# A gated-delta scan stage reordered on five engines, with one multiply moved from GpSimd to VectorE

## What is computed

```python
q = l2_norm(q) * K ** -0.5 ; k = l2_norm(k)
decay  = exp(where(incl, gcum_i - gcum_j, -inf))
a      = where(strict, (k * beta) @ k.T * decay, 0)
sol    = triangular_solve(I + a, [v * beta, k * beta * exp(gcum)])   # u, w
attn   = (q @ k.T) * decay
q_dec  = q * exp(gcum) ; k_end = k * exp(gcum_last - gcum)
# over the chunks, S = 0 at first
v_new = u - w @ S
o     = q_dec @ S + attn @ v_new
S     = S * chunk_decay + k_end.T @ v_new
```

## Time and profile before

| | us |
|---|---|
| median of 3 runs (3778.26 to 3779.26) | 3778.9 |
| the profiled execution | 3775.26 |
| its span, first to last instruction | 3773.5 |
| busy in the span: PE / DVE / ACT / POOL | 3565.7 / 1966.6 / 1510.6 / 471.2 |

### The profile page before, as it was taken

How to read it: one execution, slowest core, us unless ns; L and a number is a source line. 1 busy time by engine, 2 the same in 40 slices (tenths; PEclk the granted TensorE clock), 3 DMA queues, 4 the chain that set the end, 5 groups by cost and what they waited for, 6 DMA issues and landing times. The chain is left out here.

```text
span 3773.5 us, 49646 instructions
## 1 busy us (share of the span) xinstructions
PE 3565.7 (94%) x19794; PEld 2959.4 (78%) x19794; DVE 1966.6 (52%) x2979; ACT 1510.6 (40%) x2532; POOL 471.2 (12%) x362
## 2 busy tenths in 40 slices
PE   6999999899776789999999999999999999999998
PEld 4688888787655668888888788888888888888886
DVE  7455555467566634755455553436533444454543
ACT  3322222254644443565565642324222444442332
POOL 1000000134211000011011160120000000025021
PEclk8999999999988899999999999999999999999999
DMA  9734323332533336422223163335634555543332
GB/s 360 260 131 137 114 95 103 96 98 59 180 107 92 97 119 195 126 84 87 86 74 93 54 201 98 95 90 103 132 115 124 123 94 111 111 128 101 93 95 89
DMA packets 580503, 448.37 MB, mean 119 GB/s; under 512 B 64454, under 2 KB 500114, under 8 KB 579504
## 3 DMA queue, kind: packets, MB, share of 16 engines
q1 hardware_dynamic: 572080, 421.18, 39.6%
q10 hardware_dynamic: 6048, 19.14, 1.3%
q0 software_dynamic: 2144, 4.87, 0.4%
HBM read 387.61 MB, written 57.46 MB: 118 GB/s over the span
## 5 line engine op out<-in xcount | busy, mean ns | idle before, releaser
L2379 DVE TENSOR_TENSOR w_lo<-w,w_hi 128x512 fp32r<-128x512 f32 x429 | 291.3, 698 | 500.1 <-ACT w_hi L2372 499.9
L2372 ACT ACTIVATE w_hi<-w 128x512 fp32r<-128x512 f32 x429 | 260.9, 625 | 478.0 <-PE od_acc L2358 171.1
L4511 DVE TENSOR_TENSOR w_lo<-w,w_hi 128x512 fp32r<-128x512 f32 x260 | 232.2, 899 | 353.6 <-ACT w_hi L4404 352.2
L4370 PE MATMUL ta_acc<-u_hi,w_hi 128*128 128x512 f32 x960 | 375.2, 391 | 2.8 <-POOL u_lo L4305 1.4
L4372 PE MATMUL ta_acc<-u_hi,w_lo 128*128 128x512 f32 x960 | 373.6, 389 | 0.0
L4371 PE MATMUL ta_acc<-u_lo,w_hi 128*128 128x512 f32 x960 | 373.5, 389 | 0.0
L4404 ACT ACTIVATE w_hi<-w 128x512 fp32r<-128x512 f32 x260 | 163.5, 630 | 440.8 <-PE ta_acc L4372 433.9
L2356 PE MATMUL od_acc<-u_hi,w_hi 128*128 128x512 f32 x768 | 304.7, 397 | 0.0
L2358 PE MATMUL od_acc<-u_hi,w_lo 128*128 128x512 f32 x768 | 299.3, 390 | 0.0
L2357 PE MATMUL od_acc<-u_lo,w_hi 128*128 128x512 f32 x768 | 299.0, 389 | 0.0
L2356 PE MATMUL ev_acc<-u_hi,w_hi 128*128 128x512 f32 x608 | 250.3, 412 | 14.7 <-DVE w_lo L2379 5.1
(11 more groups left out here) (754 smaller groups left out, 8062.4 us busy)
## 6 DMA issues: line engine op xcount, KB each, us to landing
w<-in_o_w_in_dram SPq DMA_DIRECT2D x260, 256.0 KB, 6.6
w<-in_e_w_in_dram SPq DMA_DIRECT2D x144, 256.0 KB, 2.9
p_w<-in_w_in_dram SPq DMA_DIRECT2D x70, 512.0 KB, 6.2
mod_w<-in_w_ada_dram SPq DMA_DIRECT2D x32, 1024.0 KB, 11.8
w<-in_ple_gate_w_dram SPq DMA_DIRECT2D x128, 256.0 KB, 2.7
gate_w<-in_w_ada_dram SPq DMA_DIRECT2D x16, 1024.0 KB, 5.7
z_w<-in_w_in_dram SPq DMA_DIRECT2D x64, 256.0 KB, 2.9
w<-in_e_w_out_dram SPq DMA_DIRECT2D x64, 256.0 KB, 2.7
```

The costliest lines, as they stand in the source:

```text
L2372: act.activation(self.w_hi[m % self.ring][:], self.w[m % self.ring][:], ACT.Copy).then_inc(self.hi_set, 1)
L2379: eng.tensor_tensor(self.w_lo[m % self.ring][:], self.w[m % self.ring][:], self.w_hi[m % self.ring][:].bitcast(F32), ALU.subtract).then_in ...
L4370: pe.matmul(bank, hi, hi_x[:, k, :], start=(k == 0), stop=False)
L4511: dve.tensor_tensor(self.w_lo[m % RING][:], self.w[m % RING][:], self.w_hi[m % RING][:].bitcast(F32), ALU.subtract).then_inc(self.lo_set, 1)
```

## The change

The arithmetic stays the same. What changes is the place of instructions in the lists and the engine of one multiply:

- SyncE: in the opening, `scatter_in(0)` stands ahead of `gather(2)`; in each round, the q loads stand ahead of `blocks_load`.
- TensorE: in the solve, `q_sums` goes behind `level6_t`, `finish` behind `turn_v(a)`. `k_sums` goes from ahead of the scan into its step 1; queries and products of `a` from steps 2 and 3 to 3 and 4, those of `b` from step 4 to 5, and the last products of `b` behind the scan.
- ScalarE: `square_q`, `ln_q`, `norm_ln`, `norm_exp` go one place or two later in the solve, `square_k` ahead of `queries` and `inverse_q`; in the scan `decay` goes later and `turn_tri` from step 4 to step 3.
- VectorE: 18 instead of 14 triangle steps ahead of the scan, 10 instead of 6 of them ahead of `finish`; in the scan `norm_k`, `attention`, `decayed` and `turned` go later by a slot or more.
- The query multiply (`queries`, two per pair) goes from GpSimd to VectorE. The mask addition stays on GpSimd, with nothing but `identity` ahead of it in a round.

```diff
@@ -203,7 +203,7 @@
...
         TRI_STEPS = B32 - 1
-        TRI_EARLY = 14
+        TRI_EARLY = 18
         MIX_SOLVED = 56
...
@@ -343,8 +343,8 @@
...
             scatter_out(0)
+            scatter_in(0)
             gather(2)
-            scatter_in(0)
             gather(3)
...
@@ -352,13 +352,13 @@
...
                 a, b = 2 * j + 4, 2 * j + 5
+                if ahead:
+                    load_q(a)
+                    load_q(b)
                 if more:
...
                     tail.load_weights(sp, len(tail.chunks))
-                if ahead:
-                    load_q(a)
-                    load_q(b)
                 if more:
...
@@ -547,16 +547,17 @@
...
                     if ahead:
-                        if n == 2:
+                        if n == 1:
+                            k_sums(a)
+                            k_sums(b)
+                        if n == 3:
                             queries(a)
                             products(a, range(0, 4))
-                        if n == 3:
+                        if n == 4:
                             products(a, range(4, CHUNKS))
-                        if n == 4:
+                        if n == 5:
                             queries(b)
                             products(b, range(0, 4))
-                        if n == 5:
-                            products(b, range(4, CHUNKS))
                     if not more and n in (2, 4):
...
@@ -641,31 +642,30 @@
...
                 level5_y(j)
-                if ahead:
-                    q_sums(a + 2)
-                    q_sums(b + 2)
                 if more:
...
                 level6_t(j, 1)
-                if j > 0:
-                    finish(j - 1)
+                if ahead:
+                    q_sums(a + 2)
+                    q_sums(b + 2)
                 level6_y(j, 0)
...
                     tail.pe_steps(pe, TAIL)
+                if j > 0:
+                    finish(j - 1)
                 weights(j, 0)
...
                 weights(j, 1)
+                steps(j)
                 if ahead:
-                    k_sums(a + 2)
-                    k_sums(b + 2)
-                steps(j)
+                    products(b + 2, range(4, CHUNKS))
                 if more and not ahead:
...
@@ -792,11 +792,10 @@
...
                             inverse_k(a)
-                            decay(a, range(0, 3))
                         if n == 1:
...
                             inverse_k(b)
-                            decay(a, range(3, 6))
+                            decay(a, range(0, 2))
                     for d in range(2):
...
@@ -810,10 +809,10 @@
...
                         if n == 2:
-                            decay(b, range(0, 3))
-                        if n == 3:
-                            decay(b, range(3, 6))
-                    if j + 1 < PAIRS and n == 4:
+                            decay(a, range(2, 6))
+                        if n == 4:
+                            decay(b, range(0, 6))
+                    if j + 1 < PAIRS and n == 3:
                         turn_tri(j + 1)
...
@@ -900,21 +899,19 @@
...
                     tail_job(2)
-                if ahead:
-                    square_q(a + 2)
-                    square_q(b + 2)
                 level5_y(j)
...
                 if ahead:
+                    square_q(a + 2)
+                    square_q(b + 2)
+                level6_t(j, 0)
+                level6_t(j, 1)
+                if ahead:
                     ln_q(a + 2)
                     ln_q(b + 2)
-                level6_t(j, 0)
-                level6_t(j, 1)
-                if j > 0:
-                    norm_ln(j - 1)
                 level6_y(j, 0)
...
@@ -922,20 +919,22 @@
...
                 if j > 0:
-                    norm_exp(j - 1)
+                    norm_ln(j - 1)
                 weights(j, 0)
...
                     copy_v(b)
+                if j > 0:
+                    norm_exp(j - 1)
                 weights(j, 1)
                 if ahead:
-                    inverse_q(a + 2)
-                    inverse_q(b + 2)
+                    square_k(a + 2)
+                    square_k(b + 2)
                 if more:
...
                 if ahead:
-                    square_k(a + 2)
-                    square_k(b + 2)
+                    inverse_q(a + 2)
+                    inverse_q(b + 2)
                 steps(j)
...
@@ -951,12 +950,6 @@
...
 
-            def queries(hd):
-                pool.wait_ge(q_normed, hd + 1)
-                pool.wait_ge(qdec_exp, hd + 1)
-                pool.tensor_tensor(qdec[hd % 4][:], qdec[hd % 4][:], q_n[hd % 4].rearrange("p (c q) -> p c q", c=LC).unsqueeze(2)
-                                   .to_broadcast([P, LC, 2, P]), ALU.mult).then_inc(q_decayed, 1)
-
             def identity(j):
...
@@ -968,15 +961,11 @@
...
             identity(0)
-            queries(0)
-            queries(1)
             for n in range(MIX_JOBS):
...
                     identity(j + 1)
-                    queries(2 * j + 2)
-                    queries(2 * j + 3)
                 if j + 2 < PAIRS:
...
@@ -1003,6 +992,12 @@
...
                 dve.tensor_tensor(q_n[hd % 4], q_n[hd % 4], sq_q[hd % 2][:], ALU.mult).then_inc(q_normed, 1)
+
+            def queries(hd):
+                dve.wait_ge(q_normed, hd + 1)
+                dve.wait_ge(qdec_exp, hd + 1)
+                dve.tensor_tensor(qdec[hd % 4][:], qdec[hd % 4][:], q_n[hd % 4].rearrange("p (c q) -> p c q", c=LC).unsqueeze(2)
+                                  .to_broadcast([P, LC, 2, P]), ALU.mult).then_inc(q_decayed, 1)
 
...
@@ -1066,20 +1061,22 @@
...
                             if ahead and slot == 1:
-                                if n == 0 and d == 1:
+                                if n == 1 and d == 1:
                                     norm_k(a)
-                                if n == 1 and d == 1:
+                                if n == 2 and d == 0:
                                     norm_k(b)
-                                if n == 2 and d == 1:
+                                if n == 3 and d == 0:
                                     attention(a)
-                                if n == 3:
-                                    decayed(a, d)
+                                if n == 3 and d == 1:
+                                    decayed(a, 0)
                                 if n == 4 and d == 0:
+                                    decayed(a, 1)
+                                if n == 4 and d == 1:
                                     turned(a)
-                                if n == 4 and d == 1:
+                                if n == 5 and d == 0:
                                     attention(b)
-                                if n == 5:
-                                    decayed(b, d)
+                                if n == 5 and d == 1:
+                                    decayed(b, 0)
                             if slot == 0 and n < CHUNKS - 1:
...
@@ -1102,6 +1099,7 @@
...
                 if ahead:
+                    decayed(b, 1)
                     turned(b)
...
@@ -1131,6 +1129,8 @@
...
             mix.split_low(dve, mix.ring)
+            for hd in range(2):
+                queries(hd)
             for n in range(TRI_STEPS):
...
@@ -1157,14 +1157,17 @@
...
                     tail.split_low(dve, 6)
-                for n in range(6 if more else 0):
+                for n in range(10 if more else 0):
                     triangle(j + 1, n)
...
                     tail.split_low(dve, len(tail.chunks))
-                for n in range(6, TRI_EARLY if more else 0):
+                for n in range(10, TRI_EARLY if more else 0):
                     triangle(j + 1, n)
+                if more:
+                    queries(2 * j + 2)
+                    queries(2 * j + 3)
                 if ahead:
```

## The result

The changed kernel takes 3758.9 us (median of six runs, 3752.2 to 3764.5), the kernel before beside it 3779.0 (six runs). The ratio is 0.9949, with a 95% interval of 0.9936 to 0.9961. It is faster by 0.5%, and the interval lies clear of 1. The forecast was 3759.5.

What follows compares the result with a forecast made beforehand. The prediction took VectorE, last to reach the first state copies, as setting the stage's pace. Terms -1.0 - 9.8 - 2 x 5.3 + 2 = -19.4 from 3775.3 gave 3755.9, plus 3.6 for the median: 3759.5 us, range 3744 to 3773.

Steps and rivals of the forecast that it cites:

- first pair, C (absolute): End of the first pair's second state copy, predicted at 1117.4 against 1118.4 before: -1.0 us.
- C: Time point: the end of the second state copy of a pair's scan.
- second pair, T to C: Second pair up to its state copies: predicted 41.6 us against 51.4 before, -9.8.
- T: Time point: the first level-5 product of a pair on TensorE.
- scan, first and second pair: From C to the next T: predicted 33.5 us against 38.8, 5.3 gained in each of two pairs, between 0 and 7.
- third pair: Pair without mask additions: about 0.5 us worse from VectorE's work, 1.5 more from turn_tri ahead of v_end; together +2.
- The opening: Scatter ahead of gather: TensorE's first product 2 us earlier, but the first pair's triangle about 4.6 us later through queued entries.
- the hold lies mostly in a wait: Second pair: GpSimd's mask additions, expected T + 17 to T + 24, fall mostly while VectorE awaits the output norm.
- the end hangs on `turned(a)`: Rival: the scan doesn't shorten, since its end hangs on the block chain started by turned(a); 3770 us, chance 0.16.
- the additions hold nothing: Rival: the mask additions fall where VectorE is idle in both pairs; 3751.6 us, chance 0.13.
- ScalarE becomes late inside the scan: Rival: turn_tri and decay queue ahead of v_end and v_new, 10 us in each of two pairs; 3790 us, chance 0.06.
- waits only change their names: Rival: TensorE idles for VectorE as long as it did for ScalarE; 3779 us, chance 0.05.

Runs made afterwards that it cites:

- k_sums_back: Changed kernel with only the key sums put back ahead of the scan on TensorE; 3758.5 us.
- mask_out: Changed kernel with GpSimd's four mask additions of heads 4 to 7 shrunk to one chunk and two columns, so their mask is left out; 3745.6 us.
- open_old: Changed kernel with the opening's old queue order, the gather of the third head ahead of the first scatter; 3751.0 us.
- best_b: best_a with the old opening order too, gather of the third head ahead of the first scatter; 3736.0 us.
- best_a: Changed kernel with 14 early triangle steps, mask additions on VectorE, and the third pair's query multiplies at step 3 of the scan; 3743.6 us.
- tri14: Changed kernel with 14 instead of 18 triangle steps ahead of the scan; 3749.5 us.
- scan_old: Changed kernel with the scan's head work in its old order and key sums ahead of the scan, turn_tri kept at step 3; 3760.9 us.
- turn_tri4: Changed kernel with only ScalarE's turn_tri moved back from step 3 to step 4 of the scan; 3761.4 us.
- q_back: Changed kernel with query sums, squares and logarithms back in their old places and q loads behind blocks_load; 3760.3 us.

## Why the prediction was right, and where it was not

By its own terms, in the traces of before and after:

| term | predicted | measured |
|---|---|---|
| first pair, C (absolute) | -1.0 | -0.9 |
| second pair, T to C | -9.8 | -7.6 |
| scan, first and second pair | -5.3 each | -7.8, -7.8 |
| third pair | +2 | +0.6 |
| fourth pair | 0 | -0.2 |
| sum | -19.4 | -23.6 |

In the stage the trace moved by 4.2 us more than forecast, while the medians moved by 20.1. That they come so close to the sum is in part luck: two terms were off in opposite directions, and after's profiled execution is the shortest of its six, 6.7 us below their median, where that of before is 3.7 below.

**What bounds the stage** was right for the kernel after: VectorE sets C, and the removed waits were worth only what reached VectorE. k_sums_back shows it most plainly. The prediction named the key sums as lying in the wait for the copies, and putting them back costs nothing there. Before the change it held in the second pair, where VectorE made the copies without a wait. In the first pair it did not, which the prediction missed:

```profile
1112.64 0.49 DVE L1091 COPY gdn_state<-gdn_bank 128x128 f32<-128x128 f32 x2 [7.62 <-PE gdn_bank L578]
```

There VectorE stood 7.6 us for TensorE's increment, which came behind the key sums and their 4.53 us wait, so the key squares were on the path. In after VectorE has no idle time between the triangle's start and C in that pair: a later start, four more steps, the two multiplies and the additions' hold fill it, so that C barely moved.

**The first pair** held to 0.1 us in C (1117.53 for 1117.4), with the triangle at 1090.7 (for 1090.2) and two triangle instructions of 3.53 and 3.52 under the additions. mask_out finds the hold worth 6.8 in T to C; I had 6.1.

**The opening.** The first product was 2.2 us earlier for my 2, but that number varies by 4 us between executions, so it is no proof. Better is the wait ahead of it: 7.1 with the old order (before, open_old, best_b), 5.2 to 5.9 in the kernels with the new one, which is 1.2 to 1.9 and none of it reached C. What the step missed is the other queue entry: I had `turned(3)` and `keys` queued behind the scatters and counted only what that did to the triangle. `level5_x` on VectorE stands behind them too, and TensorE waited 5.33 us for it. That wait didn't show in C, which VectorE sets. The triangle's later start did: my 4.7 us for it are in the sum for C, but nowhere did I say that the step as a whole is a loss, 3.8 us of C in after and 5.3 in the lighter best_a.

**The second pair's T to C** was -7.6 for -9.8. The failed step is the sentence that "the hold lies mostly in a wait". I priced 1.8 us; mask_out gives at least 6.5. I had taken 6.5 us from issue to landing of the arguments, from a round in which SyncE paused for 8 us ahead of them. Now nothing paused, and all loads were in flight together. These are the profile's lines on the loads in the 34 us from T + 2, columns: DMAs, KB each, median us from issue to landing; first before, then after.

```profile
gdn_a_t<-s_cum_rows SPq DMA_DIRECT2D x2, 768.0 KB, 6.5
kq<-s_qkv SPq DMA_DIRECT2D x2, 384.0 KB, 5.1
```

```profile
gdn_a_t<-s_cum_rows SPq DMA_DIRECT2D x2, 768.0 KB, 11.1
kq<-s_qkv SPq DMA_DIRECT2D x2, 384.0 KB, 7.4
```

So GpSimd began at T + 20.8, not T + 17, and its 7.3 us fell on `finish`, which was ready at T + 20.95 rather than at my T + 22.5. Without the hold my layout gives 41.6 - 1.8 = 39.8, and mask_out measured 37.3. Most of that is again the output norm, which was ready at T + 20.65 there, 1.85 before my T + 22.5; VectorE's work from there to C took 16.7 us for my 17.3. The two errors, +4.7 and -2.5, leave the 2.2. Of the 7.6 that were gained, the single edits account for a part only: the query part 5.1, the query multiplies 1.9, the early steps -4.0. The rest (among it the new places of `finish`, the norm's logarithm and exponential, and the key squares) was not taken apart.

**The scan** was -7.8 for -5.3 in each pair. The chain was right: `gather(a)` started at C + 22.2 for my 22.8, and from there to T it was 8.8 for my 9.1. The term that was wrong is the 1.6 us added for TensorE's half clock after a wait. The granted clock did fall: it was 0.50, the lower of its two levels, from 1190.0 to 1193.5, behind the wait of 8.69 us (four products in 1.23 us in the row at L571 above). But in mask_out, where it was 1.00 over the first two scans, they took 32.2 and 30.8 for after's 30.7 and 31.0, so the slower products delayed nothing that can be measured. That the chain to `gather(a)` goes over VectorE is the likely reason. The reason that I gave for the lost attention wait was wrong in the main. I named the fewer triangle steps; tri14 shows that with the later products thirteen steps cost only 0.4 and 0.9 us, and scan_old that with nine steps the old order keeps 1.2 to 1.4 us of the wait. The rival that the end hangs on `turned(a)` was right about the chain and wrong about the time, since `turned(a)` came 5.3 us earlier.

**The third pair** was +0.6 for +2. The wait of 1.99 us for `v_end` behind the moved `turn_tri` is there and absent in turn_tri4, and T to C is 1.0 longer. But C to T varies by 2.5 there and T to C by 1.5, so the sum can't be told from +2.

**The rounds.** 76.9, 74.9 and 71.1 for 77, 75 and 72. The first was not quite earned: from my own C and T it should have read 1117.4 + 33.5 - 1071.4 = 79.5, as I had subtracted the T of before. The shorter scan made up for it. Two of the signs that I had named failed: in the second pair the additions held `finish` and not two triangle instructions, and in the first pair TensorE's longest wait was the 5.33 us for `level5_x`, not that for the copies.

**The rivals.** That the additions hold nothing is refuted (mask_out). That ScalarE becomes late inside the scan is refuted for the first two pairs, where C to T fell; its only trace is the 1.99 us of the third. That waits only change their names is true of the first pair up to C, where TensorE stood 17.0 us before and 16.1 after. It is refuted in the second, where it stood 20.0 and 15.3, and in both scans.

## What to carry to other kernels

Find the engine that reaches the joint last, and count only what reaches that engine: of TensorE's waits that went, the one ahead of the key sums was worth nothing once VectorE was the later engine, and the query squares' was worth 5 us only where VectorE stood for something behind it. Work that is moved ahead of a joint is paid by whoever comes last there, so four triangle steps made early cost 3.5 to 4.4 us a pair, while the scan behind took them for 0.4 to 1.0. And price a load's landing with all that is now in flight beside it, not from a round in which its queue had paused; every entry that is moved in a queue has followers on the other engines as well, all of which must be listed.

## What the runs showed of the hardware

GpSimd's two additions held VectorE's instructions with two tensor inputs in both forms that met them here. A multiply of 0.68 us took 3.84 and a scalar-tensor-tensor of 0.75 took 3.80, each until about the end of one of the additions (7.27 us for the two). The GPSIMD Engine Reference of the Trainium skill (Specifications) says that the SBUF interfaces are shared and that VectorE's instructions with two SBUF inputs contend. These rows agree, and mask_out prices it at 6.5 us in the second pair and 6.8 in the first. In q_back, where VectorE stood waiting during most of the additions, they cost it 2.6. Of the same two additions, 7.27 us for the pair on GpSimd, VectorE did the work in 3.42.

The time from issue to landing of one load grew from 6.5 to 11.1 us with its neighbours issued closer together. In the 4 us of T + 16 to T + 20 of the second pair of after the DMA engines were busy all the time and moved 410 GB/s (the last two columns; the one ahead of them is the granted clock):

```profile
1164.22:1168.22 4.00, 4.00 (x38) 4.00 (x37) 1.83 (x5) 3.31 (x8) 0.00 (x0) 1.00 1.01 410
```
